# One wait moved by a step, and one gathered tile's dot products taken from VectorE to GpSimd and ScalarE

## The reference

```python
# per token xb: 8 heads, 16 experts chosen of 16384 for each head
h = jnp.einsum('nd,nhkd->nhk', xb, u[idx])          # one dot product per chosen expert
a = jax.nn.gelu(h) * g                              # g: softmax of the 16 scores
y = jnp.einsum('nhk,nhkd->nd', a, v[idx])           # weighted sum of the experts' v rows
```

## Time and profile before

| | |
|---|---|
| median of three runs | 5125.22 us |
| the profiled execution | 5122.89 us, of it 5121.1 us span |
| experts phase, by its matmuls and sums | about 2725 to 5091 us of the span |
| TensorE busy in the whole span | 4180.8 us (82%) |
| VectorE | 3170.4 us (62%) |
| ScalarE | 1286.5 us (25%) |
| GpSimd | 626.4 us (12%) |
| mean granted clock of TensorE | 0.89 |

### The profile page before, as it was taken

The page is one execution under the profiler, slowest core; times in us unless marked ns, Lnnn a source line. Parts: engine busy times, 40 slices in busy tenths (PEclk is TensorE's granted clock), DMA queues, the critical chain, the costliest instruction groups (busy, mean ns, idle before and its releaser), DMA issues. The chain is left out here.

```text
span 5121.1 us, 61600 instructions
## 1 busy us (share of the span) xinstructions
PE 4180.8 (82%) x20219; PEld 3460.1 (68%) x20219; DVE 3170.4 (62%) x5709; ACT 1286.5 (25%) x2699; POOL 626.4 (12%) x505
## 2 busy tenths in 40 slices
PE   6999898997878863455527999999999999999996
PEld 5787566784436753454426888888888888888885
DVE  4301332111112159999986888888888888888886
ACT  2111222111112111344532222222222222222222
POOL 0000000000000000344331111111111111111110
PEclk9999676558989876788878999999999999999998
DMA  3322311102121010111127667676767667776764
GB/s 133 111 95 80 94 31 37 36 0 98 33 90 66 0 38 9 70 70 70 70 123 258 250 250 248 251 250 250 250 248 252 250 249 250 249 252 250 249 250 163
DMA packets 308267, 770.86 MB, mean 151 GB/s; under 512 B 29120, under 2 KB 170944, under 8 KB 257728
## 3 DMA queue, kind: packets, MB, share of 16 engines
q0 software_dynamic: 55360, 403.60, 20.9%
q1 hardware_dynamic: 233376, 356.77, 20.5%
q10 hardware_dynamic: 19440, 9.44, 0.6%
HBM read 681.01 MB, written 89.78 MB: 151 GB/s over the span
## 5 line engine op out<-in xcount | busy, mean ns | idle before, releaser
L2077 PE MATMUL exp_h<-exp_xh,exp_uh 128*128 128x384 f32 x2048 | 701.4, 342 | 243.7 <-ACT exp_gel L1932 193.5
L2078 PE MATMUL exp_h<-exp_xl,exp_uh 128*128 128x384 f32 x2048 | 687.3, 336 | 0.0
L2079 PE MATMUL exp_h<-exp_xh,exp_ul 128*128 128x384 f32 x2048 | 686.9, 335 | 0.0
L1900 POOL DMA_INDIRECT exp_uv<-in_peer_uv,gidx x384 | 373.6, 973 | 2009.0 <-DVE H L2010 1971.0
L2091 PE MATMUL exp_y<-exp_vh,exp_ah 128*128 128x512 f32 x1536 | 598.8, 390 | 11.5 <-DVE H L1983 11.5
L2092 PE MATMUL exp_y<-exp_vl,exp_ah 128*128 128x512 f32 x1536 | 601.0, 391 | 0.0
L2093 PE MATMUL exp_y<-exp_vh,exp_al 128*128 128x512 f32 x1536 | 601.0, 391 | 0.0
L2077 PEld LDWEIGHTS exp_h<-exp_xh,exp_uh 128*128 128x128 f32 x2048 | 386.5, 189 | 297.5 <-ACT exp_gel L1932 242.6
L2004 DVE SCALAR_TENSOR_TENSOR exp_uv<-exp_uv,exp_gx 128x1024 f32<-128x1024 f32 x384 | 469.1, 1222 | 69.3 <-DMA exp_uv<-in_peer_uv,gidx 48.5
L2010 DVE SCALAR_TENSOR_TENSOR H<-exp_uv,exp_coef,H 128x1024 f32<-128x1024 f32 x384 | 492.1, 1282 | 23.8 <-ACT exp_coef L1945 23.8
L1983 DVE TENSOR_TENSOR H<-H,exp_y 128x512 f32<-128x512 f32 x768 | 491.2, 682 | 2.5 <-PE exp_y L2093 2.4
(11 more groups left out here) (276 smaller groups left out, 6390.0 us busy)
## 6 DMA issues: line engine op xcount, KB each, us to landing
exp_u<-in_peer_u SPq DMA_DIRECT2D x128, 512.0 KB, 4.8
exp_v<-in_peer_v SPq DMA_DIRECT2D x128, 512.0 KB, 4.0
exp_w<-s_w SPq DMA_DIRECT2D x128, 384.0 KB, 3.6
out_z<-proj_zs SPq DMA_DIRECT2D x72, 256.0 KB, 2.0
proj_w<-in_w_in SPq DMA_DIRECT2D x16, 1024.0 KB, 5.4
merge_gates<-out_z SPq DMA_DIRECT2D x9, 1024.0 KB, 5.0
s_zt<-proj_zt ACTq DMA_DIRECT2D x27, 256.0 KB, 2.3
exp_uv<-in_peer_uv,gidx POOLq DMA_INDIRECT x384, 5.5
```

The source lines that it names most:

```text
L1900: pool.indirect_dma_start(out=uv[j][:, :], out_offset=None, in_=I["peer_uv"], in_offset=bass.IndirectOffsetOnAxis(ap=K["gidx"][:, e, j:j + ...
L2077: pe.matmul(hp[c][:, 0:TC], uh[s][:, n, :], xh[:, n, at], start=(n == 0), stop=False)
L2078: pe.matmul(hp[c][:, 0:TC], uh[s][:, n, :], xl[:, n, at], start=False, stop=False)
L2079: last = pe.matmul(hp[c][:, 0:TC], ul[s][:, n, :], xh[:, n, at], start=False, stop=(n == KD - 1))
```

## The change

Two things are changed, both in `phase_experts`.

1. TensorE's queue adds 6 to `y_ready` at the start. VectorE's waits on it (`add_up`) and ScalarE's last one are raised by 6 too, so they mean what they meant. ScalarE's wait ahead of `high_v` in each step keeps its number, so now it holds once `output(e - 1)` is done.
2. `dot(0)` leaves VectorE. GpSimd multiplies `exp_uv[0]` with `exp_gx` in place, behind its three gathers of the step and behind a wait for the first of them (`uv_in[0]`). ScalarE, behind `high_a(0)`, waits for it (`multiplied`), copies the product to a new tile `exp_junk` and sums it on the way into column 0 of `exp_hs`.

```diff
+        junk = sb("junk", [P, D])
...
+        multiplied = sem("ex_multiplied")
...
                         pool.indirect_dma_start(out=uv[j][:, :], ...)\
                             .then_inc(uv_in[j], 16)
+                    pool.wait_ge(uv_in[0], 16 * (e + 1))
+                    pool.tensor_tensor(uv[0][:, 0:D], uv[0][:, 0:D], gx[:, 0, :], ALU.mult).then_inc(multiplied, 1)
...
                     gelu(0)
                     high_a(0)
+                    act.wait_ge(multiplied, e + 1)
+                    act.activation(junk[:, :], uv[0][:, 0:D], ACT.Copy, accum_out=hs[s][:, 0:1]).then_inc(dotted, 1)
                     act.wait_ge(dotted, NG * (e + 1))
                     act.activation(hg[s][:, :], hs[s][:, :], ACT.Gelu_apprx_tanh)
                     gelu(1)
...
-                act.wait_ge(y_ready, NY * (NKEY - 1))
+                act.wait_ge(y_ready, NY * NKEY)
...
-                    dve.wait_ge(y_ready, NY * (out - 2) + x + 1)
+                    dve.wait_ge(y_ready, NY * (out - 1) + x + 1)
...
                     dve.drain()
-                    dot(0)
                     if not last:
                         low_u(e + 1, 1 - s)
                     dot(1)
...
                 pe.sem_inc(h_ready, 2)
+                pe.sem_inc(y_ready, NY)
```

## The result

The changed kernel takes 5143.35 us (median of 12 runs, 5131.1 to 5152.01), the kernel before 5126.23 us (median of 12 runs, 5113.84 to 5141.1). The ratio is 1.0027 with a 95% interval from 1.0016 to 1.0038: 17 us slower, which is small, but the interval does not include 1. The profiled executions took 5122.89 and 5136.06 us. So two edits, each of which takes work or a wait off VectorE, gave nothing.

A forecast was written before the change was run, and what follows sets the result against it. It took the order output, rounding of v, gelu, hidden as the bound. On VectorE, -2.24 - 1.15 + 1.20 + 2.23 = +0.04 us a step, +5 us over 127 steps, gave 5130 us; range 5065 to 5192.

The forecast's parts named there:

- The likeliest case: Whole kernel: the gains and costs on VectorE nearly cancel, giving 5110 to 5140 us; chance 0.46.
- The bound before: Expert loop: the order output, rounding of v, gelu, hidden sets the 18.34 us step; TensorE alone needs at most 16.82.
- The corrected wait, -2.24: VectorE ahead of `low_v`: the idle time for the rounding of v goes, 2.24 us a step less.
- `dot(0)` gone, -1.15: VectorE's step: the instruction that leaves it saves 1.15 us.
- The sum, +1.20: ScalarE between `high_a(0)` and `gelu(1)`: summing the product delays the chain VectorE waits for, 1.20 us a step more.
- The hold, +2.23: VectorE's `low_u` or `dot(1)`: delayed while GpSimd multiplies, 2.23 us a step more, bounds 1.65 and 3.0.
- The rest of the step: VectorE from `add_row(0)` to the next step's start: stays at 7.94 us.
- The sum of the terms: VectorE's step: all gains and costs together add 0.04 us, 18.38 instead of 18.34.
- a rival of 0.2 to 0.4 a step for a VectorE without slack: VectorE: late gathers no longer absorbed, or a longer wait for ScalarE's sum; +25 to +50 us, about 5160; chance 0.16.
- No hold at all: VectorE: GpSimd's multiplication delays nothing, but gathers make `dot(1)` and `dot(2)` wait; step 17.09, 4966 us; chance 0.06.
- Shorter and longer hold: VectorE delayed by GpSimd's multiplication for 1.65 to 2.1 us (5057 at 1.65, chance 0.20) or to 3.0 (5228, chance 0.12).

The follow-up runs named there:

- the wait alone: The kernel before with only ScalarE's corrected wait; `dot(0)` stays on VectorE, nothing new on GpSimd or ScalarE: 4931.53 us, 0.9598 of before.
- the two kernels near that limit: The kernel before with only the corrected wait, 4931.53 us, and the same with `dot(1)` put behind `low_v`, 4907.58 us.
- the third experiment: The changed kernel with ScalarE's sum and its wait for the multiplication put ahead of `high_a(0)`: 4998.68 us, 0.9732 of the kernel before.

## Why the prediction was right, and where it was off

It forecast 5130 us and no difference over 0.3%, with 5065 to 5192 as range. It is 5143, 0.27% slower, by an interval that excludes zero. The likeliest case came true with its mechanism. Its mean step, 18.38, is off by 0.05 us, and 5143 lies 3 us beyond the 5110 to 5140 that I gave to this case; the ratio times 5125.2 gives 5139, just inside. That the mean step fits so closely is in part luck: the quiet step is 0.10 shorter than forecast (18.28) and late gathers, which I had put at nothing, add 0.15.

- *The bound before.* Shown: with the wait alone the loop runs within 0.14 us a step of TensorE's limit. I had "at most 16.82" for it; its step is 16.55, and the mean step is 16.69 and 16.58 in the two kernels near that limit. In the changed kernel it idles 1.42 us a step, where I had 1.8.
- *The corrected wait, -2.24.* `low_v` has no wait left. Right.
- *`dot(0)` gone, -1.15.* Right.
- *The sum, +1.20.* `weigh(0)` to `add_row(0)` is 3031.01 - 3027.33 = 3.68 instead of 2.45, so +1.23; undone by the third experiment, which gave back 1.24.
- *The hold, +2.23.* `low_u` to `dot(1)` is 3.28 instead of 1.14, so +2.14. The multiplication takes 2.40 us; I had 2.42 from a shorter one with bf16 input, by its slope. The estimate from the Trainium skill's page "GPSIMD Engine Reference", section "Performance versus the Vector engine", was 2.30, and the measurement decides for the former. That the multiplication holds VectorE, and for its own length, is now shown from three sides: without it, with clearings in its place, and with two of it. I had left open whether `low_u` or `dot(1)` would be held: in the changed kernel it is `low_u`, in 124 of its 128 instances; with the sum earlier some steps go the other way (see the last section).
- *The rest of the step,* 7.94, is 7.89.
- *The sum of the terms* was +0.04 a step. The quiet step came out at -0.06. The mean came out at +0.08, and the late gathers are the term that was mis-sized: I had let the late gathers cost nothing "as long as the hold is there", with a rival of 0.2 to 0.4 a step for a VectorE without slack. The mean step stands 0.15 over the quiet one, which before stood at 0.01 or so: idle time ahead of `low_v` had absorbed every late gather (38.9 us of such waits between 2800 and 5040 us, and no step of TensorE over 18.41 after the first). So that rival was half true, beside my forecast and not in place of it.
- *No hold at all:* I had 17.09 a step, 159 us less, for it. With the hold taken away it is 17.76, some 86 us less, so the rival was priced too low by the same mistake, a median taken for the landing time.
- *Shorter and longer hold:* both excluded by 2.14.

## What to carry to other kernels

In this kernel, work moved from VectorE to GpSimd was not moved: a multiplication that reads SBUF, beside VectorE instructions with two SBUF inputs, comes back as a longer neighbour, and costs more than it did (2.14 us for an instruction of 1.15). Look at the longest instructions of VectorE beside GpSimd's in any phase of the trace before trusting a second engine. And when two edits are tried together, time each alone: here one is worth -4.0%, the other +1.5% by itself and +4.5% (1.0027 against 0.9598) on top of the first, since the first removes the idle time in which the second was half hidden.

## What was not expected of the hardware

- With two multiplications back to back on GpSimd, VectorE mostly does not get in between: in 116 steps `low_u` was recorded as begun 2.2 us or more before the first ended and still waited for the second. In six it did get in. There `low_u` took 3.36 us, the second multiplication 3.40 instead of 2.38, and `dot(1)` behind it was held for it. What decides between the two is not shown.

```profile
3087.20 3.36 DVE L1981 TENSOR_TENSOR exp_ul<-exp_u,exp_uh 128x1024 fp32r<-128x1024 f32 x1 [0.18 <-issue]
3090.48 3.42 DVE L2011 SCALAR_TENSOR_TENSOR exp_uv<-exp_uv,exp_gx 128x1024 f32<-128x1024 f32 x1
...
3089.42 3.40 POOL L1907 TENSOR_TENSOR exp_uv<-exp_uv,exp_gx 128x1024 f32<-128x1024 f32 x1
```

- In the step shown last of the changed kernel (3204.83), `low_u` began 0.40 us ahead of the multiplication and was held all the same (3.89 us), while the multiplication kept its 2.40. There the multiplication came straight behind a gather. In the kernel with the sum earlier, seven steps have a multiplication that first sat idle for its gather and began 0.01 to 0.78 us behind `low_u`; there `low_u` kept 1.23 us and the multiplication was stretched to 2.70 to 3.47:

```profile
2891.58 1.23 DVE L1980 TENSOR_TENSOR exp_ul<-exp_u,exp_uh 128x1024 fp32r<-128x1024 f32 x1 [0.16 <-issue]
...
2891.98 3.08 POOL L1906 TENSOR_TENSOR exp_uv<-exp_uv,exp_gx 128x1024 f32<-128x1024 f32 x1 [0.55 <-DMA exp_uv<-in_peer_uv,gidx]
```

  So it is not always the one recorded first that goes first. The Trainium skill ("SBUF — State Buffer", section "Who interferes with whom") says that the order of issue decides who blocks; by their recorded starts and these seven steps agree and the step with 3.89 us does not, but a trace shows starts, and not when each was issued.
- The clearings on GpSimd cost VectorE nothing: the step shown has 1.23 us for `low_u`, against 1.22 before.
- The gathers' median landing time is nearly the same in all kernels (5.5 to 5.7 us), but the waits for them went from 48.5 us in a kernel that could absorb them to 182.7 us in one that couldn't: how long VectorE waits is not set by the transfers alone.
